# One kernel for two blocks: a folded short transform, two PSUM banks moved, and matmuls, copies and modulation units in another order

## The reference

```python
h = h + hybrid_mixer(rmsnorm(h, norm_mix_g[l]), ...)   # w_in, pool_w, w_attn, w_pool, w_out
h = h + conv_ffn(rmsnorm(h, norm_ffn_g[l]), ...)        # w_up, w_down
```

```python
# layer 0: half of the channels through a gated convolution, half through a Fourier mixer
fg = f.reshape(b, L, FOURIER_CH // FOURIER_GROUP, FOURIER_GROUP)
f_y = jnp.fft.fftn(fg, axes=(1, 3), norm="ortho").real
# layer 1: neighbourhood attention, 16 heads, q and k normed by head
q = _heads(hx, w[:, :hd], na_q_g[j])    # _rms over the 64 channels of a head
k, v, k_c, v_c = ...
s = jnp.concatenate([s_loc, s_ctx], axis=-1); p = jax.nn.softmax(s, axis=-1)
```

## Time and profile before

| | |
|---|---|
| median of 3 runs | 1316.93 us (1316.84 to 1317.95) |
| the profiled execution | 1316.51 us |
| its span, first to last instruction | 1314.7 us |
| TensorE busy | 1297.6 us (99%) |
| VectorE busy | 873.1 us (66%) |
| ACT, POOL busy | 596.4 us (45%), 426.2 us (32%) |
| TensorE busy from 940 to 1125 us (na_in, start of na_out) | 181.76 us |

### The profile page before, as it was taken

One profiled execution on the slowest core, in us unless ns is written; L12 is line 12 of the kernel. 1 busy time (PEld: TensorE's weight loads), 2 busy tenths in 40 slices (PEclk: granted clock), 3 DMA queues, 4 the chain that ended last, 5 costly groups with the idle time before them and its releaser, 6 DMA issues.

```text
span 1314.7 us, 19888 instructions
## 1 busy us (share of the span) xinstructions
PE 1297.6 (99%) x7772; PEld 1102.3 (84%) x7772; DVE 873.1 (66%) x1303; ACT 596.4 (45%) x956; POOL 426.2 (32%) x428
## 2 busy tenths in 40 slices
PE   9999999999999999999999999999999999999999
PEld 8887989999886888788788888787777777999987
DVE  6697688999876578798433443334677665855553
ACT  6336556666643223253311233222555554766432
POOL 1473132333320002265300244011467552488200
PEclk9999999999999999999999999999999999999999
DMA  8876455555555343544434444345522321555552
GB/s 308 289 267 235 149 207 198 188 181 180 207 206 193 129 137 136 189 179 160 147 144 146 146 145 149 125 147 178 196 78 99 113 81 46 206 182 181 188 192 81
DMA packets 64476, 220.50 MB, mean 168 GB/s; under 512 B 7072, under 2 KB 10400, under 8 KB 64384
## 3 DMA queue, kind: packets, MB, share of 16 engines
q1 hardware_dynamic: 64096, 218.98, 47.3%
q10 hardware_dynamic: 288, 0.25, 0.1%
HBM read 217.73 MB, written 1.05 MB: 166 GB/s over the span
## 4 chain that ended last, share of the span: by engine, by line
PE 78%; DVE 13%; issue 5%; ACT 3%; DMA 0%; POOL 0%; SPq 0%; DVEq 0%; ACTq 0%; POOLq 0%
PE ps L615 19%; PE ps L629 18%; PE ps L627 18%; PE ps L605 7%; DVE wlo L1677 4%; PE ps L607 4%; DVE tmp L1962 2%; PE ps L1060 1%; DVE Y L1704 1%; PE ps L1087 1%; PE ps L1074 1%; ACT A L1222 1%; PE ps L727 1%; PE ps L1053 1%; DVE A L2144 1%
## 5 line engine op out<-in xcount | busy, mean ns | idle before, releaser
L615 PE MATMUL ps<-A,whi 128*128 128x256 f32 (+2 forms) x1572 | 514.8, 328 | 1.0 <-DVE A L1918 0.8
L629 PE MATMUL ps<-A,wlo 128*128 128x256 f32 (+2 forms) x1544 | 493.1, 319 | 1.1 <-DVE wlo L1677 1.1
L627 PE MATMUL ps<-A,whi 128*128 128x256 f32 (+2 forms) x1544 | 492.8, 319 | 0.2 <-DVE A L1690 0.2
L1677 DVE TENSOR_TENSOR wlo<-raw,whi 128x1024 fp32r<-128x1024 f32 x303 | 395.4, 1309 | 82.3 <-ACT whi L1197 81.9
L1197 ACT ACTIVATE whi<-raw 128x1024 fp32r<-128x1024 f32 x303 | 317.6, 1050 | 265.7 <-PE ps L629 139.8
L615 PEld LDWEIGHTS ps<-A,whi 128*128 128x128 f32 x1572 | 298.2, 190 | 48.3 <-issue 19.3
L627 PEld LDWEIGHTS ps<-A,whi 128*128 128x128 f32 x1544 | 293.4, 190 | 22.1 <-issue 1.7
L629 PEld LDWEIGHTS ps<-A,wlo 128*128 128x128 f32 x1544 | 292.9, 190 | 22.7 <-DVE wlo L1677 1.5
L2346 POOL TENSOR_TENSOR H<-tmp,H 128x256 fp32r<-128x256 f32 (+1 forms) x86 | 125.4, 1458 | 56.4 <-ACT H L1512 42.8
L605 PE MATMUL ps<-H,whi 128*128 128x512 f32 x400 | 140.4, 396 | 0.2 <-POOL H L2346 0.2
L607 PE MATMUL ps<-H,wlo 128*128 128x256 f32 x400 | 111.7, 279 | 0.5 <-DVE wlo L1677 0.4
(11 more groups left out here) (309 smaller groups left out, 1503.9 us busy)
## 6 DMA issues: line engine op xcount, KB each, us to landing
raw<-in_ada SPq DMA_DIRECT2D x96, 512.0 KB, 4.3
raw<-in_w SPq DMA_DIRECT2D x64, 512.0 KB, 4.2
raw<-in_w_up SPq DMA_DIRECT2D x44, 512.0 KB, 3.9
raw<-in_w_in SPq DMA_DIRECT2D x36, 512.0 KB, 5.6
raw<-in_w_0a SPq DMA_DIRECT2D x32, 512.0 KB, 3.6
raw<-in_w_0b SPq DMA_DIRECT2D x32, 512.0 KB, 3.5
raw<-in_na_in SPq DMA_DIRECT2D x24, 512.0 KB, 6.0
raw<-in_w_down SPq DMA_DIRECT2D x22, 512.0 KB, 4.0
```

What stands on the lines that cost most here:

```text
L615: e.matmul(o, w_hi, ah, start=k == 0, stop=False)
L627: e.matmul(o, w_hi, al, start=False, stop=False)
L629: m = e.matmul(o, w_lo, ah, start=False, stop=last)
L1677: e.tensor_tensor(wlo[i % NRAW][:, :cols], raw[i % NRAW][:, :cols], plain(whi[s % NHI][:, :cols]), SUB).then_inc(S("wlo").sem, 1)
```

## The change

Nothing is computed otherwise but for the short transform: its table `fold` keeps 33 cosines and 31 sines of each group, made on POOL, and VectorE unfolds the rest from the symmetry (`unfolded`). The other edits:

- the index heads come one unit earlier, the selection has two rounds in each of the units 16 to 23, and the masks come after 19 and 23;
- `pool_w` 1 takes bank 5, and `w_attn` 0 waits for chunk 36 of w_in only;
- one modulation unit of VectorE goes from w_down's unit 16 to ab_in's unit 9;
- in ab_out's steps on VectorE the residual (`gated`) comes ahead of the modulation's copy (`written`);
- in na_in's chunks of k and v with attention work in their middle (5, 7, 8, 10, 12, 13, 15, 16, 18, 19, 21, 22 and 23; `early`), the small work for the chunk before stands behind that attention work, and no longer at the end;
- na_out's chunk 3 has its high parts ahead of its low ones (`out_high`, `out_low`).

```diff
-MOD_AFTER = {"w_down": (1, 3, 16), "ab_in": (5, 6, 7, 10, 12, 13, 14), "ab_out": range(6), "w1_0a": (*EVEN, 5, 11),
+MOD_AFTER = {"w_down": (1, 3), "ab_in": (5, 6, 7, 9, 10, 12, 13, 14), "ab_out": range(6), "w1_0a": (*EVEN, 5, 11),
...
-INDEX_MM = {12 + i: i for i in range(8)}
+INDEX_MM = {11 + i: i for i in range(8)}
 INDEX_SUM = {u + 1: job for u, job in INDEX_MM.items()}
-INDEX_LARGEST = {16: [(0, 1)], 17: [(0, 2)], 18: [(0, 2)], 19: [(0, 2)], 20: [(0, 1)], 21: [(1, 2)], 22: [(1, 2)],
-                 23: [(1, 2)], 24: [(1, 2)]}
-INDEX_MASK = {20: 0, 24: 1}
+INDEX_LARGEST = {u: [(u // 20, 2)] for u in range(16, 24)}
+INDEX_MASK = {19: 0, 23: 1}
...
-APART = {("w_in", 3): 3, ("w_in", 4): 5, ("w_in", 5): 7, ("pool_w", 3): 4, ("na_out", 3): 4, ("na_out", 4): 5, ("na_out", 5): 7}
+APART = {("w_in", 3): 3, ("w_in", 4): 5, ("w_in", 5): 7, ("pool_w", 1): 5, ("pool_w", 3): 4, ("na_out", 3): 4, ("na_out", 4): 5, ("na_out", 5): 7}
...
+    fold = h32("fold", 128, 57344).rearrange("p (h m) -> p h m", h=2)
...
-            elif name == "pool_w" and n == 3:
+            elif name == "pool_w" and n in (1, 3):
                 w.wait_ge(S("sc_x"), 8)
+            elif (name, n) == ("w_attn", 0):
+
+                w.wait_ge(S("resc_w_in"), 37)
...
             c = n - 1
             if 0 <= c < 4:
                 w.wait_ge(S("ab"), c + 1)
-                w.wait_ge(S("seqs"), 16)
+                w.wait_ge(S("fold"), 4)
+                if c >= 2:
+                    w.wait_ge(S("ab_yt"), c - 1)
+                else:
+                    w.wait_ge(S("nx_v"), 1)
+                    w.wait_ge(S("ng_v"), 1)
                 for t4 in range(4):
-                    f = 4 * c + t4
-                    if f >= 2:
-                        w.wait_ge(S("ab_yt"), f - 1)
-                    else:
-                        w.wait_ge(S("nx_v"), 1)
-                        w.wait_ge(S("ng_v"), 1)
-                    e.matmul(ps[4 + f % 2][:, 0:256], F[:, c, 128 * t4:128 * t4 + 128], seq_const("cs64"),
-                             start=True, stop=True).then_inc(S("ab_f").sem, 1)
+                    m = e.matmul(ps[4 + c % 2][:, 128 * t4:128 * t4 + 128], F[:, c, 128 * t4:128 * t4 + 128],
+                                 fold.rearrange("p h m -> p (h m)"), start=True, stop=True)
+                m.then_inc(S("ab_f").sem, 1)
             written("ab_in", n)
...
         linear("ab_in", 512, lambda k: (Ahi[:, k], Alo[:, k]), n2_hi, n2_lo, during=during_ab)
-        w.wait_ge(S("ab_yt"), 16)
+        w.wait_ge(S("ab_yt"), 4)
+        w.wait_ge(S("yt0"), 1)
+        w.wait_ge(S("seqs"), 16)
...
 
+        def early(n):
+
+
+            return 2 <= n < 24 and NA_CHUNKS[n][0] != "q" and any(x is not None for x in attend2(n - 1))
+
         def during_na(n):
-            m = n - 1
+            if not early(n):
+                from_chunk(n - 1)
+            mod_summed("na_in", n)
+            written("na_in", n)
+
+        def from_chunk(m):
+
             if 0 <= m < 24:
                 if norm2(m):
                     j, _, T = norm2(m)
@@ -1101,8 +1118,6 @@
                         t = e.transpose(ps[6][:, 128 * t4:128 * t4 + 128], tmp[4][:, 128 * t4:128 * t4 + 128], ident)
                     t.then_inc(S("v2_tr").sem, 1)
                     bank6[0] = ("v2", NA_CHUNKS[m][1] + 1)
-            mod_summed("na_in", n)
-            written("na_in", n)
...
 
+        def midway_na(n):
+            after_na(n - 1)
+            if early(n):
+                from_chunk(n - 1)
+
         first_two("na_in", (512, 256), lambda k: (Ahi[:, k], Alo[:, k]), ready("na_hi", 2), ready_low("na_lo", "na_lp", 2))
         during_na(1)
         linear("na_in", lambda n: 256 if NA_CHUNKS[n][0] == "q" else 512, lambda k: (Ahi[:, k], Alo[:, k]), ready("na_hi", 2),
-               ready_low("na_lo", "na_lp", 2), during=during_na, midway=lambda n: after_na(n - 1), begin=2)
+               ready_low("na_lo", "na_lp", 2), during=during_na, midway=midway_na, begin=2)
 
...
 
+        def out_high(n, pairs):
+
+            s, o = SPLIT_AT["na_out", n], bank_of("na_out", n)[:, :256]
+            bank_free("na_out", n)
+            w.wait_ge(S("whi"), s + 1)
+            for k in pairs:
+                w_hi = whi[s % NHI][:, 128 * k:128 * k + 128]
+                w.wait_ge(S("O2_hi"), k + 1)
+                e.matmul(o, w_hi, Ohi[:, k], start=k == 0, stop=False)
+                w.wait_ge(S("O2_lo"), k + 1)
+                e.matmul(o, w_hi, Olo[:, k], start=False, stop=False)
+
+        def out_low(n, pairs):
+
+            s, o = SPLIT_AT["na_out", n], bank_of("na_out", n)[:, :256]
+            low_ready(s)
+            for k in pairs:
+                e.matmul(o, wlo[SPLIT[s] % NRAW][:, 128 * k:128 * k + 128], Ohi[:, k], start=False, stop=False)
+
 
...
             if u == 25:
-                out_part(3, range(2))
+                out_high(3, range(6))
             if u == 26:
                 for n in range(3):
                     out_part(n, (6,))
-        out_part(3, range(2, 7))
+        out_high(3, (6,))
+        out_low(3, range(7))
         for n in range(4):
...
 
+        def unfolded(x):
+
+            w.wait_ge(S("ab_f"), x + 1)
+            o = ps[4 + x % 2].rearrange("p (t h m) -> p t h m", t=4, h=2)
+            cosines, sines = [YT[:, :, x, 128 * i:128 * i + 128].rearrange("p t (h m) -> p t h m", h=2) for i in range(2)]
+            e.tensor_copy(cosines[:, :, :, 0:33], o[:, :, :, 0:33])
+            e.tensor_copy(cosines[:, :, :, 33:64], o[:, :, :, 31:0:-1])
+            e.tensor_copy(sines[:, :, :, 1:32], o[:, :, :, 33:64])
+            e.tensor_scalar(sines[:, :, :, 33:64], o[:, :, :, 63:32:-1], -1.0, None, MUL, ALU.bypass).then_inc(S("ab_yt").sem, 1)
+
         def final_norm(c):
...
                 n, c = i, i % 4
                 if 1 <= n < 5:
-                    for t4 in range(4):
-                        f = 4 * (n - 1) + t4
-                        w.wait_ge(S("ab_f"), f + 1)
-                        e.tensor_copy(YT[:, t4, n - 1, :], ps[4 + f % 2][:, 0:256]).then_inc(S("ab_yt").sem, 1)
+                    unfolded(n - 1)
                 written("ab_in", n)
...
             if what == "chunk":
+                gated("ab_out", "about_r", 0, 0, i, 512, None)
                 written("ab_out", i)
-                gated("ab_out", "about_r", 0, 0, i, 512, None)
 
...
         for c in range(22):
             a, b = tmp[2 * c % 4][:, :256], tmp[(2 * c + 1) % 4][:, :256]
+            if c == 16:
+                w.wait_ge(S("seqs"), 16)
+                for h in range(2):
+                    for i, first, n in ((0, 64 * h, 33), (33, 129 + 64 * h, 31)):
+                        e.tensor_scalar(fold[:, h, i:i + n], seq_const("cs64", first, n), 1.0, 1.0, MUL, MUL).then_inc(S("fold").sem, 1)
...
 
+        w.wait_ge(S("mm"), end_of("w_down"))
+        e.memset(YT[:, :, :, 128:256:32], 0.0).then_inc(S("yt0").sem, 1)
```

## The result

The changed kernel is slower by a small amount: median 1319.98 us of 14 runs, beside 1317.22 of 14 runs of the kernel before on the same chip. The ratio is 1.0019, with a 95% interval of 1.0012 to 1.0025. The forecast was 1316.6. The time lies in the stated range, but the move has the other sign: 2.8 us up where 0.3 down was forecast.

The account below looks back on a forecast made before the run. TensorE, busy 1297.6 of 1314.7 us, was taken as the bound. Terms -3.9 + 4.0 - 1.5 - 0.9 + 0 - 0.3 + 3.0 - 0.7 gave -0.3 on 1316.5; with 0.4 to the median, 1316.6, range 1312.0 to 1320.8.

Parts of the forecast that it names:

- rival 3: The 4 us stop at 47 us drops TensorE's clock, losing up to 2.9 us: 1319.5, chance 0.14.
- Rival 4: In the neighbourhood attention nothing is absorbed, as VectorE moves with TensorE: +3.4 on the forecast, 1320.0, chance 0.13.
- Index heads one unit earlier: First index matmuls, moved behind w_in's unit 11, make TensorE wait for POOL's ik from 47.20 to 51.2 us: +4.0.
- The -1.5 at 111 us: TensorE's wait of 1.52 us for the first probabilities goes, with the selection over a unit sooner: -1.5.
- Head sums in the middle: In na_in, sums behind the attention's matmuls at thirteen places add stops: net 3.35, taken as +3.0, ends -1 and +6.4.
- what the existing waits absorb: In na_in, five waits for VectorE's read of a sum ahead of the next scores shrink as TensorE comes later: -3.4.
- the gross, 6.75: New stops in na_in before absorption: 4.25 at five chunks behind scores, 1.2 at chunk 7, 1.3 for transposes of v.
- the 0.35 taken off for fewer changes between kinds of matmul: In na_in, net 3.35 was taken as 3.0, since fewer changes may save a little; no row priced that.
- The short transform: Four groups of matmuls in ab_in, 128 columns in place of 256, take 0.91 us each in place of 1.89: -3.9.
- w_attn: Its first chunk no longer waits 0.83 us for the second pooled low part: -0.9, ends 0.5 and 1.0.
- na_out: Fourth chunk's high matmuls fill a 1.05 us wait for low weights, about 0.5 comes back: -0.7, ends 0 and -1.2.
- ab_out: Residual ahead of small modulation operations on VectorE, so the square TensorE waited 0.3 us for is there: -0.3.

Follow-up runs that it names:

- e9: Changed kernel with eight useless matmuls of 256 columns in the stop ahead of the first pair of index heads: 1317.75 us, 0.9997 of the kernel before.
- e8: Kernel before with the short transform's change alone, all other edits left out: 1313.51 us, ratio 0.9967.
- e3: Changed kernel with na_in's head sums and transposes of v back at the chunk's end, the stop kept: 1316.53 us, 0.9994 of the kernel before.
- e1: Changed kernel with all four index tables (matmuls, sums, selection rounds, masks) as before: 1314.64 us, 0.9979 of the kernel before.
- e2: Changed kernel with only the index matmuls and their sums back at 12 to 19, new selection rounds and masks kept: 1314.35 us, 0.9981 of the kernel before.
- e5: Changed kernel with index matmuls back at 12 to 19 and head sums and transposes at the chunk's end: 1310.23 us, 0.9940 of the kernel before.
- e7: Changed kernel with index matmuls at 12 to 19 and the middle only at chunks 7, 8, 12, 13, 16, 19, 22, 23: 1313.93 us, ratio 0.9972.
- e4: Changed kernel with the first pair of index heads behind unit 11's two modulation units, not ahead: 1318.08 us, 1.0009 of the kernel before.
- e10: Kernel before with three useless matmuls of 256 columns in its 1.5 us stop near 110 us: 1318.59 us, ratio 1.0001.

## Why the forecast was wrong, step by step

**The step that failed on sign: leaving the lower clock out of the sum.** The forecast said "By the rule the sum would be some 3 us higher if the stop is long enough for it", and made it rival 3 with a chance of 0.14 at 1319.5, because no row showed a fall in the middle. Its mechanism is the one found: all 14 runs have a mean clock under 1.000, the fall cost 2.4 us in the trace where the rival's working gave up to 2.9, and e9 shows that it goes when the stop is filled. With the stop filled the time is that of the kernel before (0.9997), so without this term no loss is measured. The evidence against it was weak: that no stop up to 1.5 us was followed by a fall in one execution says nothing on a stop of 4, and e8 shows that it was not even true of 1.5 us in every execution. That 1319.98 lies so close to the rival's 1319.5 is in part luck, since three other terms were off as well, by +1.2, +1.2 and -0.9 (below). Rival 4 gave 1320.0 by a mechanism that the runs exclude: it had nothing absorbed in na_in, and 3.7 us were.

**Index heads one unit earlier.** Right in its mechanism: forecast 4.0, measured 3.9 (3.0 in e3's trace). The -1.5 at 111 us came as a wait removed, but two waits for low weights came ahead of it, 0.3 and 0.4 at 98.6 and 106.2 us, and they cost 1.3 in the account. My working looked at VectorE's rounds only for the mask and not for what they may push back, its low parts. e1 against e2 puts the whole gain at 0.3.

**Head sums in the middle.** This term was 3.0 and is 3.3 to 3.5 (e3), 4.1 (e2 less e5) or 4.2 (the traces). The places were right, and so was what the existing waits absorb: forecast 3.4, measured 3.7. The score groups lost 5.1 us in the kernel before and lose 1.4 now, in two groups:

```profile
957.76 1.98 PE L1066 MATMUL ps<-k,q 64*128 64x512 f32 x4
997.15 1.71 PE L1066 MATMUL ps<-k,q 64*128 64x512 f32 x4
1061.19 1.13 PE L1066 MATMUL ps<-k,q 64*128 64x512 f32 x4
```

What was too small is the gross, 6.75 where the starts give 8.1: 4.6 for the five stops (forecast 4.25), 2.0 at chunk 7 (1.2) and 1.6 for the transposes of v (1.3). Chunk 7's wait for the square is 1.66 us here and 1.00 in e7, where no stop stands at chunk 5 before it, so the places could not be priced one by one; why the square comes later stays open. And the 0.35 taken off for fewer changes between kinds of matmul did not come: a moved sum costs the same in its new place. The 3.4 was read from a row of the weight loads (it begins with PEld). TensorE's own row shows much less:

```profile
PE ps L1060 <- DVE tmp L2206: 1.2, 2, 0.7
```

That row would have misled: the starts show that the larger figure is the nearer one.

**The short transform** was mis-sized, on the good side: -4.77 against -3.9. I priced a record of 128 columns by the long transform's average of 0.114; from start to start a group of eight takes 0.81 with the change back to the projections, and in the account 1.19 less than before. The lower copies and POOL's table cost nothing, as said.

**The small ones held.** w_attn -0.95 (forecast -0.9), na_out -0.7 (-0.7, with the new wait of 0.3 for POOL's last low part), ab_out -0.35 (-0.3). The DMA wait ahead of ab_in stayed, at 1.3 in place of 0.9; in the traces of e1 to e9 it is 0.3 to 1.3. None of these was undone by itself.

**The sum** with what the runs showed, against the kernel before: -4.8 (transform) + 3.9 (stop) + 2.4 (clock) - 0.3 (selection) - 0.95 (w_attn) - 0.35 (ab_out) + 4.2 (na_in) - 0.7 (na_out) = +3.4, beside 2.8 between the medians and 4.0 between the profiled executions.

## What to carry to other kernels

A matmul moved ahead of its input costs the stop and then the clock: here 3.9 us of waiting were 6.3 us of time, and eight useless matmuls in the gap gave 2.4 of them back. When you count on an existing wait to absorb a new one, measure it from start to start against an undisturbed group of the same matmuls: TensorE's idle row had 1.2 us, that of its weight loads 3.4, and 5.1 were lost, of which 3.7 came back. And test the parts of a bundle one by one: this one held 6.8 us of gain, hidden by two edits that lost 9.6 (2.8 over the kernel before against 6.8 under it).

## What the runs showed of the hardware

- The clock fell in the traces with stops of 3.9, 3.0 and 2.9 us, and 35 of 36 runs of these kernels (the changed one, e3 and e4) have a mean clock under 1.000. After 1.5 us it fell in one trace (e8) and not in others. With the stop of 3.9 us it had fallen before the stop ended (0.51 from 49.50 us on); with that of 2.9 it fell 1.6 us behind its end.
- Eight matmuls that nothing reads, put into the stop of 3.9 us, kept the clock at 1.000 in 11 of 11 runs (e9), and the same work behind it took 4.47 us in place of 6.88.
- The clock also fell to 0.58 over 4 us (960 to 964 in e10) behind a stop of 0.7 us, the longest of the 40 us before; nothing in the trace tells why there.
- Two matmuls of 64 rows with 512 columns, ready together, are multiplied side by side: their four records take 1.13 us, as long as the two of one that stands alone (1.12).
- VectorE's copies out of PSUM with a reversed innermost axis take as long as forward ones: 406 ns for 248 elements.
- POOL's addition of 128 x 256 values in the rotation takes 0.72 to 0.80 us or 1.6, and ik's took 1.59 in the changed kernel's trace and 0.72 in e3's, behind the same code.
